# One core, two transformer blocks: the order of VectorE's gate multiplies and low-part subtractions behind the convolution

## The reference

```python
h = rmsnorm(x, norm_mix_g[l])
proj = jnp.einsum('bsd,dc->bsc', h, w_in[l])
u, v, bg, cg, xs, ga, gb = jnp.split(proj, split_at, axis=-1)
...
a = spatial_gating(gelu(u), rmsnorm(gelu(v), norm_v_g[l]), w_s[l], b_s[l])
c = bg * causal_dwconv(cg * xs, conv_w[l])        # width 3, along the tokens
m = sigmoid(ga + b_gate_a) * (a @ w_proj_a) + sigmoid(gb + b_gate_b) * (c @ w_proj_b)
x = x + m @ w_out
x = x + relu(rmsnorm(x) @ w_ff1) ** 2 @ w_ff2
```

## Time and profile before

| | |
|---|---|
| median of 3 runs | 1040.22 us |
| profiled execution, its own time | 1041.88 us |
| its span, first to last instruction | 1040.1 us |
| VectorE busy | 508.4 us, 49% |
| ScalarE busy | 407.7 us, 39% |
| gate multiplies L1738 | x4, 680 ns median |
| subtractions L1740 | x4, 693 ns median, 2.9 us idle before them in all |
| copies L1245 | x4, 632 ns median |
| mean DMA rate over the span | 315 GB/s |

### The profile page before, as it was taken

The page is one execution under the profiler, slowest core; times in us unless marked ns, Lnnn a source line. Parts: engine busy times, 40 slices in busy tenths (PEclk is TensorE's granted clock), DMA queues, the critical chain, the costliest instruction groups (busy, mean ns, idle before and its releaser), DMA issues.

```text
span 1040.1 us, 13693 instructions
## 1 busy us (share of the span) xinstructions
PE 1017.4 (98%) x5588; PEld 681.8 (66%) x5588; DVE 508.4 (49%) x714; ACT 407.7 (39%) x643; POOL 21.7 (2%) x42
## 2 busy tenths in 40 slices
PE   9999999999999999999999999999999999999986
PEld 6888878888999999899887544344444444344332
DVE  5676677887987755657876321121112111211112
ACT  7734643535544444574873222122222222222212
POOL 1100000010000000100000000000000000000000
PEclk9999999999999999899999999999999999999998
DMA  9987548977788844365468799999999999999993
GB/s 332 391 281 243 181 153 287 326 268 244 256 311 294 296 179 163 98 243 163 162 244 332 296 415 421 420 422 421 421 421 421 421 421 421 422 421 420 422 420 142
DMA packets 86179, 327.89 MB, mean 315 GB/s; under 512 B 5744, under 2 KB 5904, under 8 KB 61408
## 3 DMA queue, kind: packets, MB, share of 16 engines
q1 hardware_dynamic: 84912, 323.98, 80.6%
q0 software_dynamic: 1200, 2.98, 0.9%
HBM read 325.88 MB, written 1.05 MB: 314 GB/s over the span
## 4 chain that ended last, share of the span: by engine, by line
PE 51%; DMA 5%; DVE 1%; issue 0%; ACT 0%; ACTq 0%
PE bank L1024 19%; PE bank L1047 9%; PE bank L1066 3%; DMA e_whi<-in_w_expert_up 3%; PE bank L992 3%; DMA raw<-in_w_expert_up 3%; PE bank L584 2%; PE bank L587 2%; PE bank L1033 2%; PE bank L590 2%; PE bank L552 1%; PE bank L555 1%; PE bank L558 1%; PE bank L1006 1%; PE bank L1008 1%; PE bank L765 1%
## 5 line engine op out<-in xcount | busy, mean ns | idle before, releaser
L1626 DVE TENSOR_TENSOR wlo<-raw,whi 128x2048 fp32r<-128x2048 f32 x87 | 199.1, 2289 | 86.9 <-ACT whi L1121 86.5
L1121 ACT ACTIVATE whi<-raw 128x2048 fp32r<-128x2048 f32 x87 | 165.9, 1912 | 95.3 <-PE bank L558 35.9
L1024 PE MATMUL bank<-es,XT 128*64 128x512 f32 x496 | 148.8, 596 | 1.9 <-DMA raw<-in_w_expert_up 1.9
L2260 DVE SCALAR_TENSOR_TENSOR YS<-bank,wsl,gate2q 128x512 f32<-128x512 f32 x32 | 24.0, 751 | 216.9 <-PE bank L1047 216.9
L1024 PE MATMUL bank<-raw,XT 128*64 128x512 f32 x336 | 101.6, 596 | 1.8 <-DMA raw<-in_w_expert_up 1.8
L555 PE MATMUL bank<-wlo,hh 128*128 128x512 f32 x224 | 87.5, 391 | 1.6 <-DVE wlo L1626 1.4
L552 PE MATMUL bank<-whi,hh 128*128 128x512 f32 x224 | 88.1, 393 | 0.4 <-ACT whi L1128 0.4
L1024 PEld LDWEIGHTS bank<-es,XT 128*64 128x64 f32 x496 | 44.2, 137 | 66.4 <-issue 64.7
L558 PE MATMUL bank<-whi,hl 128*128 128x512 f32 x224 | 87.3, 390 | 0.0
L1615 DVE SCALAR_TENSOR_TENSOR ada_acc<-raw,silu_c,ada_acc 128x512 f32<-128x512 f32 x96 | 72.0, 750 | 2.5
L2251 DVE TENSOR_TENSOR SG<-SG,bank 128x256 f32<-128x256 f32 x32 | 13.5, 421 | 121.8 <-ACT SG L1534 111.3
(11 more groups left out here) (381 smaller groups left out, 1866.0 us busy)
## 6 DMA issues: line engine op xcount, KB each, us to landing
raw<-in_w_in SPq DMA_DIRECT2D x41, 1024.0 KB, 5.7
raw<-in_w_ff SPq DMA_DIRECT2D x32, 1024.0 KB, 5.3
es<-in_w_expert_up SPq DMA_DIRECT2D x32, 1024.0 KB, 24.2
es<-in_w_expert_gate SPq DMA_DIRECT2D x30, 1024.0 KB, 25.9
es<-in_w_expert_down SPq DMA_DIRECT2D x29, 1024.0 KB, 22.6
raw<-in_w_ada SPq DMA_DIRECT2D x24, 1024.0 KB, 6.0
raw<-in_w_expert_gate SPq DMA_DIRECT2D x22, 1024.0 KB, 22.1
raw<-in_w_expert_up SPq DMA_DIRECT2D x20, 1024.0 KB, 19.0
```

Source lines behind the costliest of these rows:

```text
L1024: m = e.matmul(b[64 * w:64 * w + 64, :], K.XT[j // 4 % 2][:, k, j % 4, :], K.weights(halves[w])[:, 512 * c:512 * c + 512], start=k == 0, s ...
L1121: e.activation(whi[n % RING][:, :], raw[h.raw][:, :], ACT.Copy).then_inc(S["hi"], 1)
L1626: e.tensor_tensor(wlo[n % RING][:, :], raw[h.raw][:, :], whi[n % RING][:, :].bitcast(F32), ALU.subtract).then_inc(S["lo"], 1)
```

## The change

For each chunk pair k the gate multiply of pair k + 1 is issued on VectorE ahead of the subtraction of pair k. The instructions, their operands, semaphores and increments are the same.

```diff
-    for k in range(4):
+
+    def gated(k):
         o = slice(2 * k, 2 * k + 2)
         e.wait_ge(S["turned"], TURNED["b"] + k + 1)
         e.tensor_tensor(K.y[:, o, :], K.y[:, o, :], two(K.at[f"bT{k}"][0]), ALU.mult).then_inc(S["cT"], 1)
+
+    gated(0)
+    for k in range(4):
+        if k < 3:
+            gated(k + 1)
+        o = slice(2 * k, 2 * k + 2)
         e.wait_ge(S["x_hi"], SPLIT["c"] + k + 1)
         e.tensor_tensor(K.cl[:, o, :], K.y[:, o, :], K.ch[:, o, :].bitcast(F32), ALU.subtract).then_inc(S["x_lo"], 1)
     lo(23)
```

## The result

| | before | changed |
|---|---|---|
| median of 20 runs each | 1041.62 us | 1039.68 us |
| lowest and highest | 1040.11, 1045.04 | 1037.95, 1042.36 |
| ratio | 1 | 0.9978 (95% interval 0.997 to 0.9987) |
| profiled execution, its span | 1040.1 us | 1037.8 us |

The ratio says that the change is worth 0.22%, some 2.3 us (1.4 to 3.1); the two medians differ by 1.94. The prediction had said 2.0 us and 1038.2. The time is 1039.68 and not 1038.2 because the median of before rose from 1040.22 in three runs to 1041.62 in twenty.

The account below looks back on a forecast made before the run. TensorE, busy 98%, was taken as the bound, delayed 1.33 + 0.67 = 2.00 us by two waits on VectorE's remainders. 1041.88 less 2.00 gives 1039.88; with the run median 1.66 lower, 1038.2 us, range 1036.2 to 1041.0.

Parts of the forecast that it names:

- The lead: VectorE's last gate subtraction starts 2.69 us sooner, because the next multiply fills the idle time during ScalarE's copy.
- The signs: Expected in the changed trace: subtractions without idle time, except about 0.03 us at the first and 0.15 to 0.2 before the last.
- The bound of 0.5 us for ScalarE working beside VectorE: Up to 0.5 us of lead lost if four copies and multiplies each stretched by a tenth; 0 was taken.
- The two waits: TensorE's waits on VectorE's weight remainders, 1.03 us before half 23 and 0.38 before half 24, both go.
- The three deadlines: TensorE wants the remainders for half 23 at 146.38, half 24 at 151.82 and half 28 at 174.54; all would be met.
- The waits' full price: Counted in TensorE's eight-matmul steps, the waits at halves 23 and 24 cost 1.33 + 0.67 = 2.00 us.
- To the end: All 2.00 us reach the kernel's end, since the expert weights' DMA stream starts by TensorE's progress and shifts with it.
- Rival A: Only the wait at half 23 goes, the one at half 24 stays; gain 1.33 us or less, 1038.9 us, chance 0.07.
- a lead of 1.8 us needed at both places: VectorE must come at least about 1.8 us sooner at halves 24 and 28; below that TensorE gains little more than the lead.
- 0.5%: Smallest difference from no change a measurement could tell, 5.2 us: faster below 1035.0 us, slower above 1045.4.
- C: Moved pauses make TensorE's low-clock stretch near 436 run twice as long, adding 3.4 us: 1041.6 us, chance 0.05.
- D: TensorE's clock does not fall near 436 and 3.4 us are given back: 1034.8 us, chance 0.04.

Follow-up runs that it names:

- `lo(23)` first, old order: Kernel before with lo(23), its modulation tile and hi(23) ahead of the four multiply-subtract pairs, pairs in old order; run twice, ratios to before 1.001 and 0.9997.
- `lo(23)` first, new order: Changed kernel with lo(23), its modulation tile and hi(23) moved ahead of the pairs; ratio to before 0.9995 (0.9983 to 1.0007).
- before, one filler: Kernel before with one unused VectorE memset of 640 columns added ahead of the modulation tile and lo(23); one run, 1042.21 us.
- before, three fillers: Kernel before with three unused VectorE memsets of 640 columns added ahead of the modulation tile and lo(23); ratio to before 1.0043.
- transposes of x early: Changed kernel with the last eight transposes of x in ff0 done one chunk (twelve matmuls) earlier on TensorE; ratio to before 0.9975.
- before, two fillers: Kernel before with two unused VectorE memsets of 640 columns added ahead of the modulation tile and lo(23); one run, 1045.46 us.
- changed, again: The changed kernel repeated without further edits, beside the kernel with lo(23) first in the old order; ratio to before 0.9978 (0.9963 to 0.9993).
- before, four fillers: Kernel before with four unused VectorE memsets of 640 columns added ahead of the modulation tile and lo(23); ratio to before 1.0041.

## Why the prediction was right

**The lead.** Forecast 2.69 us, measured 2.78. The sum took 0.11 us from the end of each multiply to ScalarE's copy, from the first pair (134.87 to 134.97). At the later pairs it is 0.03 to 0.04, as it is in the kernel before, so `ch3` and the last subtraction came a little sooner. The signs named an idle time of about 0.03 us before the first subtraction; the prediction's own schedule has 0.16 there (135.47 to 135.63), and so has the trace. The bound of 0.5 us for ScalarE working beside VectorE was not used: the copies took 632 ns as before, the multiplies 679.

**The two waits.** Both went, as worked out. The three deadlines, with the 0.24 us of later start taken off, are 146.38, 151.82 and 174.54, exactly the forecast ones. The waits' full price, 1.33 + 0.67 from eight steps of 0.68 us, was right, where the waits list shows only 1.03 + 0.38: M fell by 2.00.

**To the end.** The stream of expert weights followed, in the changed kernel and in the ones made slower. The span fell by 2.3 us. Of that, 2.00 is M. The changed execution came to the transposes 0.24 us later, so the stretch behind M must have given some 0.5 us more; 0.26 of it is there by the weight issue, and the rest in the tail. It is within what executions scatter, and I don't ascribe it.

**What was mistaken in it.** Rival A's price. If the first wait is cured alone, TensorE runs into the second, and the gain is what VectorE's lead at the second place gives and not 1.33 us. Here VectorE came 0.65 us sooner there, and M fell by 0.61 and 0.66. The forecast itself had the right rule, a lead of 1.8 us needed at both places: with 1.40 the second wait stayed. The prediction also took 0.5% for the smallest difference that a measurement of this kernel can tell. With twenty runs of each the interval was 0.17% wide, and the gain of 0.22% lies clear of it.

**Rivals C and D, the clock.** The stretch of the earlier trace rows in the changed kernel:

```profile
430.00:434.00 4.00, 3.57 (x25) 3.52 (x24) 1.84 (x9) 0.70 (x4) 1.33 (x3) 0.76 0.40 67
434.00:438.00 4.00, 4.00 (x20) 4.00 (x20) 4.00 (x11) 2.71 (x7) 0.00 (x0) 0.50 0.01 4
438.00:442.00 4.00, 4.00 (x32) 4.00 (x31) 4.00 (x9) 4.00 (x9) 0.00 (x0) 0.89 0.00 0
```

Lost are 4 x 0.24 + 4 x 0.50 + 4 x 0.11 = 3.4 us, as before. Neither came to pass here. In the first run with `lo(23)` ahead half of D did, at the same code:

```profile
434.00:438.00 4.00, 3.42 (x22) 3.16 (x22) 3.54 (x9) 2.74 (x7) 0.00 (x0) 0.76 0.04 6
438.00:442.00 4.00, 4.00 (x30) 4.00 (x29) 4.00 (x11) 3.33 (x10) 0.00 (x0) 0.81 0.00 0
```

That is 1.7 us lost where the repetition lost 3.4, as did the other profiles of this study. Its W is 1.0 shorter than there, at the same M; the clock is the likely cause, not a tested one. It happens to a kernel from run to run and is not a property of the change. The Trainium skill ("TensorE: Matmul & The Clock Gate", Part 1) says that the window over which activity is judged is "free-running"; these two traces of one kernel agree, with 1.7 us of clock lost in the one, and in the other 4 x 0.17 + 4 x 0.50 + 4 x 0.18 = 3.4 (from 432 to 444).

## What to carry to other kernels

Two engines that alternate over small pieces (multiply here, copy there, subtract here) leave the first one idle for each handover; one piece of lookahead in its queue takes most of the idle time away (here 2.78 us of it). A second piece took away the rest, 0.4 us, which TensorE did not need. What that is worth is read at the consumer: add up its waits with what they cost in steps of its own, find the next deadlines behind them, and check the lead at each one, since a wait that is cured alone comes back at the next. Where the effect is smaller than the scatter of whole runs, measure a distance inside the trace. It shows what the edit did there; what whole runs make of it can still differ, as the kernel with `lo(23)` first in the new order does.

## What the runs showed of the hardware

**Pauses and the clock.** In the three kernels with two to four fillers the low stretch behind the pause was 3.4, 6.8 and 3.4 us long, with no order by the pause's length, and cost 1.6 to 2.8 us beyond the pause (M less the waits). The waits that the change removed, 1.03 and 0.38 us, left the clock full. But the length of a pause alone does not decide it. Some waits of TensorE in the profiles, and what the clock did behind them:

| TensorE's wait, us | kernel, end of the wait | clock behind it |
|---|---|---|
| 1.61 | before, one filler, 148.03 | stays full |
| 1.84 | changed, 1004.98 | stays full |
| 1.95 | `lo(23)` first, old order, 1005.46 | falls |
| 1.95 | before, three fillers, 1011.06 | stays full |
| 2.22 | transposes of x early, 1004.38 | stays full |
| 2.38 | before, two fillers, 149.19 | falls |
| 2.69 | before, three fillers, 981.12 | falls |
| 2.85 | before, two fillers, 1010.70 | stays full |
| 2.93 | `lo(23)` first, new order, 975.39 | falls |
| 3.20 | before, three fillers, 149.70 | falls |
| 3.31 | changed, again, 1006.19 | falls |
| 3.99 | before, four fillers, 149.83 | falls |

Two of them, each with TensorE's matmul behind the wait and the stretch around it. Behind 1.95 us the clock fell, behind 2.85 it did not:

```profile
1005.46 0.61 PE L1024 MATMUL bank<-e_wlo,XT 128*64 128x512 f32 x1 [1.95 <-DMA e_whi<-in_w_expert_up]
1004.00:1008.00 4.00, 2.54 (x8) 1.00 (x10) 1.00 (x2) 0.63 (x1) 0.00 (x0) 0.77 1.02 424
```

```profile
1010.70 0.61 PE L1024 MATMUL bank<-e_wlo,XT 128*64 128x512 f32 x1 [2.85 <-DMA e_whi<-in_w_expert_up]
1010.00:1012.00 2.00, 1.30 (x6) 0.57 (x8) 0.03 (x1) 0.00 (x0) 0.00 (x0) 1.00 1.04 434
```

And in the stretch of the earlier trace rows the clock fell with no wait of TensorE over 0.43 us in the fifteen us in front. So a pause that cost nothing in one profile is no promise for the next.

**Scatter at the end.** In the changed kernel's second profile the last weights let TensorE wait 3.31 us at 1006 (1.84 in the first), and the clock was low for about 3.4 us:

```profile
1004.00:1008.00 4.00, 1.81 (x6) 0.66 (x8) 0.69 (x1) 0.35 (x1) 0.00 (x0) 0.74 1.01 420
1008.00:1012.00 4.00, 4.00 (x21) 1.39 (x17) 0.00 (x0) 0.00 (x0) 0.00 (x0) 0.83 1.01 420
```

Sixteen matmuls took 5.20 us there and 3.65 in the first, and the span was 1039.6 us (1037.8) with an M that differs by 0.04. Over the 20 runs of the changed kernel the time goes with the mean granted clock (correlation -0.80): the fastest, 1037.95 us, had 0.996, the slowest, 1042.36, had 0.992.
